# A decoder step on one core: sampled tokens' attention inside the prompt attention's loop, by pairs of heads

## The chip, the cores and the metric

The kernel runs on one core of one Trainium2 chip. TensorE (PE) multiplies and transposes, VectorE (DVE), ScalarE (ACT) and GpSimd (POOL) work elementwise, and DMAs are asked for by SyncE (SP) or, after the change, by ACT too. The time is the device time of one execution in microseconds; three executions are shown. An operand in float32 is split into a high and a low part in a rounded format (fp32r), and a product is three matmuls (high by high, low by high, high by low).

## The reference, cut to what matters

Two token sets go through the same trunk of two layers: a prompt (1024 tokens) and samples (8 sequences of 8 new tokens, each with 1024 past tokens in 8 pages of 128). Layer A is a gated short convolution. Then shared keys and values are made, and layer B attends with 16 heads of 64. For the samples, the past keys and values stand in a pool of pages that a table points into:

```python
k_past = cache_k[page_table].reshape(db, -1, N_HEADS, HEAD_DIM)     # 8 x 1024 x 16 x 64
s_past = einsum('bqhd,bkhd->bhqk', q, k_past) * scale + cn_q + rest # cn, rest: sums of log f
s_new  = einsum('bqhd,bkhd->bhqk', q, k_new) * scale + cn_q - cn    # causal, 8 x 8
p = softmax(concatenate([s_past, s_new])); o = p[..., :P] @ v_past + p[..., P:] @ v_new
```

The prompt's attention is causal over 1024 keys with a bias from the cumulated log forget values. Both results are gated by silu(z), go through w_out and a last gated feed, and a norm.

## The kernel before, in words

TT = 1088 columns are 1024 prompt tokens and 64 sampled ones, and a dense tile (one 128-wide slice of a weight matrix against all 1088 columns) is 24 pieces of three matmuls each: three column blocks (BLK) by eight slices of the inner dimension.

- **Convolution stage** (46 to about 425 us): `conv_layer` runs over j = 0 to 7 with four tiles each (t = 0 to 3). For each tile SP loads the raw weights (`load`, L312), POOL multiplies by the norm's gain (`gain`, L504), ACT rounds to w_hi (L991), DVE subtracts to w_lo (L1301). Weights have two buffers. w_hi of the next tile waits until the tile before the present one is finished. At t = 2 ACT also computes silu of the three blocks (L1052), after DVE has taken them out of PSUM. After that come w_out's eight tiles and the first feed.
- **Prompt attention** (757 to 1424.5 us): a loop over the 8 pairs of heads, each in two halves (one head each). The order of work is written out by hand in `STEPS`, which PE, ACT and DVE walk alike: ("S", qb) scores of query block qb against its keys, ("D", n) n dense pieces of the next pair's projections, ("N", i) transposes of the new keys or values, ("T", g, kb) transposes of probabilities, ("V", g, kb) product with the values. Each half has 48 dense pieces. S runs on PSUM banks 3 to 5, T and N on 5 and 6, V on 7, dense on 0 to 2. After S: DVE takes the row maximum (L1505), ACT the exponential (L1128), DVE the reciprocal (L1510), POOL multiplies (`normalise`, L536); T is followed by ACT's p_hi (L1136) and DVE's p_lo (L1516). In the last pair only 24 dense pieces are left of 96.
- **Sampled attention** (1424.5 to 1667.4 us): a loop over the 8 sequences (`sample_batch`). Pages are loaded whole from the cache (128 rows of 4 KB, L444 and L436) to `Kpages` and `Vpages`. For one sequence PE transposes 64 blocks of keys (L844), multiplies them with the queries (`s_scores`, L866; a float32 matmul stands as two instructions in the trace), adds the biases by 16 matmuls of 512 columns (`s_bias`, L855 to L858), transposes the probabilities (L895, L892) and multiplies by the values (`s_values`, L911). ACT and DVE take keys out of PSUM (L1238, L1632). There is no dense work beside this.
- **The end**: DVE's last product with the gate (L1687), the split of the result into high and low parts, w_out's eight tiles, the second feed, the norm and the stores.

SP's DMAs are asked for in program order on one queue; a wait on SP holds everything behind it.

## Time and profile before

| | us |
|---|---|
| median of 3 executions | 1923.3 (1920.92 to 1925.39) |
| profiled execution, its own time | 1923.05 |
| its span, first to last instruction | 1921.3 |
| PE busy | 1766.8 (92%) |
| PE weight loads busy | 1617.0 (84%) |
| DVE, ACT, POOL busy | 888.1 (46%), 692.3 (36%), 265.5 (14%) |
| mean granted clock of PE | 0.965 |

Times of rows are from the span's start. A timeline row is start, duration, engine, line, operation, output<-input and count; "[0.31 <-DVE ...]" is idle time before it and what ended it. SPq is SyncE's queue.

### The profile page before, as it was taken

To read this page: it belongs to the slowest core of one execution; us is meant where nothing else is said; L and a number is where in the kernel's file an instruction comes from. 1 tells how busy PE (TensorE), PEld (TensorE's weight loads), DVE (VectorE), ACT (ScalarE), POOL (GpSimd) and SP (SyncE) were. 2 spreads that over 40 slices of the span, in tenths; PEclk is the share of its full clock that TensorE was granted. 3 is DMA by queue.
4 is the path that set the end of the run, shared out by engine and by line. 5 is a ranking of instruction groups with operands and counts; after the bars stand their busy time and mean duration, and the time that the engine had idled before them with its cause. 6 is when DMAs were issued, how large, how long until landed. Compare 5 with 4: busy or idle time off the path is not lost.

```text
span 1921.3 us, 33244 instructions
## 1 busy us (share of the span) xinstructions
PE 1766.8 (92%) x11874; PEld 1617.0 (84%) x11874; DVE 888.1 (46%) x1433; ACT 692.3 (36%) x1150; POOL 265.5 (14%) x233
## 2 busy tenths in 40 slices
PE   6999999999999769999999999999779999899997
PEld 5999999999999659888888888888656666699997
DVE  4433333343253474555555555555444344423443
ACT  5111111121142234565655556555423233302332
POOL 4111111100000022222212222221100000000010
PEclk8999999999999889999999999999869999899998
DMA  4111111111211213110102111010326868721102
GB/s 140 46 46 45 45 45 45 45 33 44 75 42 30 104 13 103 35 57 23 56 23 78 46 34 56 24 56 23 134 94 268 304 258 329 279 75 49 41 27 93
DMA packets 163427, 161.61 MB, mean 84 GB/s; under 512 B 18188, under 2 KB 140172, under 8 KB 163126
## 3 DMA queue, kind: packets, MB, share of 16 engines
q1 hardware_dynamic: 163382, 161.03, 25.3%
q8 instruction: 26, 0.43, 0.1%
q14 instruction: 19, 0.16, 0.0%
HBM read 137.20 MB, written 23.80 MB: 84 GB/s over the span
## 4 chain that ended last, share of the span: by engine, by line
PE 74%; DVE 9%; ACT 5%; issue 5%; DVEq 3%; ACTq 2%; POOL 1%; DMA 0%; SPq 0%; POOLq 0%
PE PS L577 14%; PE PS L579 14%; PE PS L578 14%; PE PS L738 4%; PE PS L740 4%; PE PS L739 3%; PE PS L797 3%; PE PS L844 3%; PE PS L785 2%; DVE small L1505 2%; PE PS L911 2%; PE PS L768 2%; PE PS L866 2%; DVE pTl L1516 1%; PE PS L769 1%
## 5 line engine op out<-in xcount | busy, mean ns | idle before, releaser
L577 PE MATMUL PS<-Hhi,w_hi 128*128 128x364 f32 (+1 forms) x1536 | 511.9, 333 | 38.3 <-DVE Hlo L1351 35.1
L579 PE MATMUL PS<-Hhi,w_lo 128*128 128x364 f32 (+1 forms) x1536 | 509.7, 332 | 0.0
L578 PE MATMUL PS<-Hlo,w_hi 128*128 128x364 f32 (+1 forms) x1536 | 507.3, 330 | 0.0
L577 PEld LDWEIGHTS PS<-Hhi,w_hi 128*128 128x128 f32 x1536 | 293.9, 191 | 42.5 <-issue 29.1
L578 PEld LDWEIGHTS PS<-Hlo,w_hi 128*128 128x128 f32 x1536 | 293.1, 191 | 0.0
L579 PEld LDWEIGHTS PS<-Hhi,w_lo 128*128 128x128 f32 x1536 | 292.7, 191 | 0.0
L738 PE MATMUL PS<-Hhi,w_hi 128*128 128x364 f32 (+1 forms) x768 | 274.0, 357 | 0.1
L740 PE MATMUL PS<-Hhi,w_lo 128*128 128x364 f32 (+1 forms) x768 | 252.6, 329 | 0.0
L739 PE MATMUL PS<-Hlo,w_hi 128*128 128x364 f32 (+1 forms) x768 | 251.9, 328 | 0.0
L991 ACT ACTIVATE w_hi<-w_raw 128x1024 fp32r<-128x1024 f32 (+1 forms) x97 | 105.7, 1090 | 371.3 <-PE PS L579 368.1
L504 POOL TENSOR_TENSOR w_raw<-w_raw,GT 128x1024 f32<-128x1024 f32 x65 | 127.1, 1957 | 697.9 <-DMA w_raw<-in_w_kv 386.3
L1301 DVE TENSOR_TENSOR w_lo<-w_raw,w_hi 128x1024 fp32r<-128x1024 f32 (+1 forms) x97 | 125.2, 1290 | 79.3 <-ACT w_hi L991 76.4
L1516 DVE TENSOR_TENSOR pTl<-PS,pTh 128x512 fp32r<-128x512 f32 x192 | 103.6, 555 | 123.1 <-ACT pTh L1136 120.8
L1128 ACT ACTIVATE Pb<-PS,small 128x128 f32<-128x128 f32 (+7 forms) x128 | 94.9, 742 | 160.8 <-DVE small L1505 160.8
L536 POOL TENSOR_SCALAR Pb<-Pb,small 128x128 f32<-128x128 f32 (+7 forms) x128 | 95.6, 751 | 377.9 <-DVE small L1510 377.9
L738 PEld LDWEIGHTS PS<-Hhi,w_hi 128*128 128x128 f32 x768 | 147.0, 191 | 0.7 <-DVE w_lo L1301 0.2
L739 PEld LDWEIGHTS PS<-Hlo,w_hi 128*128 128x128 f32 x768 | 145.9, 190 | 0.0
L740 PEld LDWEIGHTS PS<-Hhi,w_lo 128*128 128x128 f32 x768 | 144.8, 189 | 0.0
L1136 ACT ACTIVATE pTh<-PS 128x512 fp32r<-128x512 f32 x192 | 89.9, 488 | 97.0 <-PE PS L785 93.7
L1505 DVE TENSOR_REDUCE small<-PS 128x1 f32<-128x128 f32 (+7 forms) x128 | 95.7, 749 | 37.2 <-PE PS L771 36.9
L797 PE MATMUL PS<-pTh,VS 128*128 128x512 f32 x192 | 73.6, 383 | 35.2 <-DVE pTl L1516 35.2
L785 PE MATMUL PS<-ident,Pb 128*128 128x128 f32 x576 | 94.7, 285 | 6.7 <-POOL Pb L536 6.7
(254 smaller groups left out, 2303.4 us busy)
## 6 DMA issues: line engine op xcount, KB each, us to landing
Kpages<-in_cache_k SPq DMA_DIRECT2D x64, 512.0 KB, 5.8
Vpages<-in_cache_v SPq DMA_DIRECT2D x64, 512.0 KB, 5.6
w_raw<-in_w_in_a SPq DMA_DIRECT2D x64, 256.0 KB, 3.0
w_raw<-in_w_ple_gate SPq DMA_DIRECT2D x16, 512.0 KB, 3.7
w_raw<-in_w_kv SPq DMA_DIRECT2D x32, 256.0 KB, 3.2
w_raw<-in_w_in_b SPq DMA_DIRECT2D x32, 256.0 KB, 3.2
parked_x<-X SPq DMA_DIRECT2D x8, 544.0 KB, 5.0
X<-parked_x SPq DMA_DIRECT2D x8, 544.0 KB, 7.8
```

What stands on the lines that cost most here:

```text
L504: g.tensor_tensor(w, w, GT[:, :, r:r + 1].to_broadcast([P, KC, P]), ALU.mult).then_inc(sems["w_gained"], 1)
L577: mm(out, wh, hi[:, k, s:e], start=(k == 0), stop=False)
L578: mm(out, wh, lo[:, k, s:e], start=False, stop=False)
L579: last = mm(out, wl, hi[:, k, s:e], start=False, stop=(k == nk - 1))
L738: mm(out, wh, Hhi[:, k, s:e], start=(k == 0), stop=False)
L739: mm(out, wh, Hlo[:, k, s:e], start=False, stop=False)
L740: last = mm(out, wl, Hhi[:, k, s:e], start=False, stop=(k == KC - 1))
L785: last = tp(PS[:, 5 + kb % 2, qi * P:(qi + 1) * P], Pb[:, off:off + P], ident[:, :])
L797: last = mm(PS[:, 7, q0 * P:512], VS[:, kb, hh, :], x[:, kb % 2, q0 * P:512], start=(kb == 0 and x is pTh), stop=(kb == nkb - 1 and x is pTl))
L1301: tt_(wlo[:, par, 0:nk, :], raw[:, par, 0:nk, :], f(whi[:, par, 0:nk, :]), ALU.subtract).then_inc(sems["w_split"], 1)
L1505: ve.reduce_max(small[:, qb:qb + 1], score_bank(qb)[:, 0:n], AXX, negate=True).then_inc(sems["rowmax"], 1)
L1516: tt_(pTl[:, kb % 2, q0 * P:512], PS[:, 5 + kb % 2, q0 * P:512], f(pTh[:, kb % 2, q0 * P:512]), ALU.subtract).then_inc(sems["p_lo"], 1)
```

## The change

1. The loop over the 8 sequences is gone. Each turn of the prompt's loop over pairs is now: half 0, a **key phase**, half 1, a **value phase**. These serve one pair of heads for all 8 sequences, so that 8 x 2 x 8 = 128 rows of scores stand in one PSUM tile of 1088 columns.
2. The 96 dense pieces of a pair are shared out anew: half 0 has 40, the key phase 12, half 1 has 38, the value phase 6.
3. The pages are first copied within DRAM, sorted by pair: keys_by_pair and values_by_pair. These 128 copies (512 KB each, in runs of 512 B) are asked for by ACT, four in each of the 32 tiles of the convolution stage, before that tile's w_hi. The loop then reads them through a ring of three buffers of 512 KB: 8 units of keys and 8 of values in a pair.
4. The biases become one matmul over 50 rows. These rows are put together by small DMAs into the tile KA for each pair.
5. The weights' buffers have another layout (parity inside), rsb and rs2 share space, the log forget values are reordered on POOL, and the end takes the prompt's result from DRAM into Hlo.

```diff
-STEPS = [("S", 0), ("D", 2), ("N", 0), ("N", 1), ("D", 1), ("S", 1), ("D", 2), ("N", 2), ("D", 1), ("S", 2), ("D", 3),
-         ("S", 3), ("D", 3), ("S", 4), ("D", 4), ("T", 0, 0), ("T", 0, 1), ("S", 5), ("D", 5), ...
+HALF0 = half_steps((2, 1, 2, 2, 3, 4, 5), (0, 1), (6, 1, 4))
+HALF1 = half_steps((2, 1, 2, 2, 3, 4, 5), (1, 2), (5, 1, 3))
+KEY_D = [1, 1, 2, 1, 2, 1, 2, 2]
+VALUE_D = [2, 4]
+RING = 3
...
+            def copy_pages(j, t):                                   # ACT
+                for pg in (2 * t, 2 * t + 1):
+                    v = act.value_load(pt[0:1, bass.ds(PAGES * j + pg, 1)], min_val=0, max_val=last_page)
+                    rows = bass.ds(v * PAGE, PAGE)
+                    by_pair = lambda x: x[rows, :].rearrange("t (j c) -> t j c", j=NPAIR)
+                    act.dma_start(dk[:, pg // 2 * P:(pg // 2 + 1) * P, bass.ds(j, 1), pg % 2, :]..., by_pair(ck)).then_inc(sems["pages_in"], 16)
+                    act.dma_start(dv[:, pg * P:(pg + 1) * P, bass.ds(j, 1), :]..., by_pair(cv)).then_inc(sems["pages_in"], 16)
             def conv_layer(j, last, first=False):
                 for t in range(4):
+                    copy_pages(j, t)
                     if last and t == 3:
...
+            def load_unit(j, u):                                    # SP
+                if u >= RING:
+                    if u - RING < PAGES:
+                        sp.wait_ge(sems["s_kturn1"], 8 * j + u - RING + 1)
+                    else:
+                        sp.wait_ge(sems["s_vused"], 8 * j + u - RING - PAGES + 1)
...
+                sp.dma_start(dst, src).then_inc(sems[f"r_in{SLOT[u]}"], 16)
+            def keys(j, more):                                      # SP, between half0 and half1
+                for u in range(RING, PAGES):
+                    load_unit(j, u)
+                if more:
                     load_b1(j, 3, 1)
...
+                for u in range(PAGES, PAGES + RING):
+                    load_unit(j, u)
+            def values(j, more):                                    # SP, after half1 and its store of yT
+                for u in range(PAGES + RING, 2 * PAGES):
+                    load_unit(j, u)
+                if more:
+                    sp.wait_ge(sems["s_vused"], 8 * j + 8)
+                    for u in range(RING):
+                        load_unit(j + 1, u)
...
+            def key_phase(j, more):                                 # PE
+                q = Q_KEYS
+                s_bias(j)                                           # 2 matmuls, 50 rows x 512 columns
+                for u in range(PAGES):
+                    s_turn(j, u)                                    # 8 transposes
+                    if u:
+                        s_scores(j, u - 1)                          # 4 matmuls of 256 columns
+                    dense(j, q, KEY_D[u], more)
+                    q += KEY_D[u]
+                s_scores(j, PAGES - 1)
+                s_new(j)                                            # 1 + 8 matmuls of 64 columns
+            def value_phase(j, more):
+                pe.wait_ge(sems["exp"], START["exp"] + 16 * j + 16)
+                pe.wait_ge(sems["s_exp"], j + 1)
...                                                                  # 8 + 1 transposes of Ps
+                dense(j, Q_VALUES, VALUE_D[0], more)
+                pe.wait_ge(sems["s_pt0"], 2 * j + 2)
+                for pg in range(PAGES):
...
+                    pe.wait_ge(sems[f"r_in{SLOT[u]}"], 16 * (USES[SLOT[u]] * j + USE[u] + 1))
+                    for g_ in range(4):
+                        last = mm(PS[32 * g_:32 * g_ + 32, 6, 0:256], PsT[:, pg, 32 * g_:32 * g_ + 32],
+                                  ring[:, SLOT[u], 256 * g_:256 * g_ + 256], start=(pg == 0), stop=False)
+                    last.then_inc(sems["s_vused"], 1)
...                                                                  # 8 matmuls with the new values
+                dense(j, Q_VALUES + VALUE_D[0], VALUE_D[1], more)
+                pe.wait_ge(sems["s_osb"], j + 1)
+                tp(PS[:, 7, 0:P], Osb, ident[:, :]).then_inc(sems["s_yturn"], 1)
...
                 if i == 0:                                          # PE, turn_part
                     pe.wait_ge(sems["staged"], 3 * j + (1, 3)[t])
+                    if t == 0 and attend:
+                        pe.wait_ge(sems["s_exp"], j)
...
+            # ACT: key_phase takes banks 3 out to KT, then Exp over 1088 columns; value_phase takes out PsT
+            # DVE: key_phase takes bank 4 out to KT, then reduce_max over 1088 columns; value_phase PsT, Osb, zsS
-            sample_batch(b, more) on PE, ACT, DVE, value_pages and Kpages loads on SP: removed
```

## Rows read from the trace of the kernel before

**Rows 1.** Busy time by stage; columns: stretch, its length, engines, clock, DMA share, GB/s.

```profile
46.00:515.00 469.00, 462.48 (x2765) 461.56 (x2765) 175.15 (x265) 64.61 (x79) 55.68 (x29) 0.99 0.16 47
757.10:1348.70 591.60, 558.14 (x3434) 505.19 (x3433) 334.16 (x601) 341.75 (x620) 134.56 (x139) 1.00 0.15 43
1348.70:1424.50 75.80, 55.18 (x246) 43.22 (x244) 34.87 (x71) 32.50 (x67) 11.97 (x16) 0.73 0.24 85
1424.50:1667.40 242.90, 220.00 (x2672) 148.05 (x2672) 102.80 (x238) 73.44 (x153) 0.00 (x0) 0.98 0.75 283
1095.10:1179.60 84.50, 79.69 (x492) 72.14 (x491) 47.80 (x87) 49.07 (x89) 19.48 (x20) 1.00 0.15 45
```

**Rows 2.** SP's timeline: stores of yT at the ends of pairs 0 and 6.

```profile
841.59 0.39 SPq L409 DMA_DIRECT2D parked_y<-yT  x1
...
1348.69 0.39 SPq L409 DMA_DIRECT2D parked_y<-yT  x1
```

**Rows 3.** PE's timeline: dense pieces, one every three matmuls.

```profile
1102.98 0.32 PE L738 MATMUL PS<-Hhi,w_hi 128*128 128x364 f32 x1
...
1103.47 0.33 PE L738 MATMUL PS<-Hhi,w_hi 128*128 128x364 f32 x1
```

**Rows 4.** PE's timeline in the sampled attention: transposes and scores of keys.

```profile
1504.38 1.07 PE L866 MATMUL PS<-KT,qc 128*32 128x256 f32 x16 [0.31 <-DVE KT L1632]
...
1526.97 1.09 PE L844 MATMUL PS<-ident,Kpages 128*128 128x128 f32 x8
1527.99 0.64 PE L866 MATMUL PS<-KT,qc 128*32 128x256 f32 x8
```

**Rows 5.** The whole timeline there: new keys, values, biases.

```profile
1506.10 0.32 PE L880 MATMUL PS<-knT,qc 128*32 128x64 f32 x8
...
1514.13 1.95 PE L911 MATMUL PS<-Vpages,PsT 128*32 128x128 f32 x64
...
1519.45 0.48 PE L855 MATMUL PS<-RT,pick 128*128 128x512 f32 x1
...
1524.73 0.44 PE L919 MATMUL PS<-ident,Osb 128*128 128x128 f32 x2
```

**Rows 6.** ACT's and DVE's timelines there: maximum, exponential.

```profile
1507.67 1.22 DVE L1658 TENSOR_REDUCE small<-PS 128x1 f32<-128x1024 f32 x1
1509.15 1.12 ACT L1252 ACTIVATE Ps<-PS,small 128x1024 f32<-128x1024 f32 x1 [0.46 <-DVE small L1660]
```

**Rows 7.** One half: exponentials on ACT, the scores on PE that wait for them.

```profile
1112.45 1.01 ACT L1128 ACTIVATE Pb<-PS,small 128x896 f32<-128x896 f32 x1 [2.41 <-DVE small L1505]
1113.61 0.50 PE L768 MATMUL PS<-KA,QA 128*128 128x512 f32 x1
```

**Rows 8.** Who waited on PE in 1095.1 to 1179.6: us, times, longest.

```profile
PE PS L797 <- DVE pTl L1516: 4.3, 5, 1.8
```

**Rows 9.** The tile Vpages: DMA (512 KB, 4 KB rows) from issue to landing.

```profile
DMA to landing us min/median/max: 3.2/5.6/7.8
```

**Rows 10.** DMA rate in 735.8 to 741, stores of KN in 512 B runs (40 slices).

```profile
GB/s 0 0 0 0 0 0 0 114 303 295 288 295 288 288 291 288 295 288 288 288 252 217 178 32 0 0 0 0 0 0 0 0 0 0 0 0 126 0 0 0
```

**Rows 11.** DMA rate in 841.5 to 847, at its end weights in 512 B runs.

```profile
GB/s 0 0 0 0 0 0 0 417 447 387 387 477 328 387 238 477 268 71 127 182 253 313 320 246 209 257 328 335 350 350 343 331 339 346 346 343 324 343 320 331
```

**Rows 12.** Line 354, eight stores of 544 KB asked for in a row: ns min/median/max.

```profile
L354 SPq DMA_DIRECT2D parked_x<-X x8: 345/1194/1237, 656.1 to 662.8; - x8
```

**Rows 13.** ACT's timeline in the convolution stage: silu and w_hi of successive tiles.

```profile
77.41 0.51 ACT L1052 ACTIVATE scrZ<-scrZ 128x360 f32<-128x360 f32 x1 [2.85 <-DVE scrZ L1379]
...
88.79 1.06 ACT L991 ACTIVATE w_hi<-w_raw 128x1024 fp32r<-128x1024 f32 x1 [9.93 <-PE PS L579]
100.75 1.06 ACT L991 ACTIVATE w_hi<-w_raw 128x1024 fp32r<-128x1024 f32 x1 [10.89 <-PE PS L579]
```

**Rows 14.** Stretches of 5 us in the last pair (columns as in rows 1).

```profile
1369.00:1374.00 5.00, 1.17 (x6) 1.03 (x7) 2.98 (x7) 3.04 (x4) 2.14 (x2) 0.68 0.95 274
...
1389.00:1394.00 5.00, 3.41 (x13) 2.51 (x13) 1.83 (x6) 1.45 (x4) 1.77 (x3) 0.50 0.00 0
```

More of the change, by code:

```diff
@@ L418, in _ @@
             load_b1(0, 3)
+            sp.wait_ge(sems["out_dma"], 32)
+            sp.wait_ge(sems["pages_in"], 16 * 2 * DB * PAGES)
+            for u in range(RING):
+                load_unit(0, u)
             store_kv(0, 0)
@@ L799, in pv_step, with dense @@
                 last.then_inc(sems["pv"], 1)
+            def dense(j, q, n, more):
+                for x in range(q, q + n):
+                    if more or x < 24:
+                        dense_piece(j, *divmod(x, PIECES))
             def half_pair(j, half, more):
-                p = 0
-                for step in STEPS:
+                q = (0, Q_HALF1)[half]
+                for step in (HALF0, HALF1)[half]:
                     if step[0] == "S":
@@ L1186, in beside @@
                 i = 2 * half + p // 24
+                if not more and half == 1 and p == 10:
+                    w_hi(N_B2 % 2, B_B2 - 3, loaded(N_B2))
                 if p % 24 == 16 and more:
@@ L1206, in beside, with dense @@
                     evacuate(j, half, *leaves[half][p], attend)
+            def dense(j, q, n, more):
+                for x in range(q, q + n):
+                    beside(j, *divmod(x, PIECES), True, more)
             def half_pair(j, half, more):
-                p = 0
-                for step in STEPS:
+                q = (0, Q_HALF1)[half]
+                for step in (HALF0, HALF1)[half]:
                     if step[0] == "S":
@@ new lines, in _ @@
+            with act.Fori(0, NPAIR - 1) as j:
+                pair(j, True)
+            pair(NPAIR - 1, False)
+            act.wait_ge(sems["o_done"], START["o_done"] + 4 * NPAIR)
+            act.wait_ge(sems["s_out"], START["s_out"] + NPAIR)
+            act.wait_ge(sems["y_back"], 16 * (KC - 1))
+            af(Hhi[:, :, SEQ:], zsS[:, :, :], ACT.Copy)
+            for k in range(KC):
+                af(Hhi[:, k, 0:SEQ], f(Hlo[:, k, 0:SEQ]) if k < KC - 1 else yT[:, 0:SEQ], ACT.Copy).then_inc(sems["h_hi"], 1)
@@ L1588, in beside, with dense @@
                     ve.tensor_copy(at_pair(zsS, j).rearrange("p a n -> p (a n)"), zf[:, SEQ:])
+            def dense(j, q, n, more):
+                for x in range(q, q + n):
+                    beside(j, *divmod(x, PIECES), True, more)
             def half_pair(j, half, more):
-                p = 0
-                for step in STEPS:
+                q = (0, Q_HALF1)[half]
+                last_sum = False
+                for step in (HALF0, HALF1)[half]:
                     if step[0] == "S":
@@ L1605, in half_pair @@
                     if step[0] == "D":
-                        for _ in range(step[1]):
-                            beside(j, half, p, True, more)
-                            if p == 29:
-                                row_sum(j, half, 7)
-                            p += 1
+                        early = 3 if last_sum else step[1]
+                        dense(j, q, early, more)
+                        if last_sum:
+                            row_sum(j, half, 7)
+                            last_sum = False
@@ new lines, in half_pair, with key_phase @@
+                        dense(j, q + early, step[1] - early, more)
+                        q += step[1]
+            def key_phase(j, more):
+                q = Q_KEYS
+                for u in range(PAGES):
+                    ve.wait_ge(sems["s_kturn1"], 8 * j + u + 1)
+                    if u >= 2:
+                        ve.wait_ge(sems["s_score"], 8 * j + u - 1)
+                    ve.tensor_copy(KT[:, u % 2, 2:4, :].rearrange("p g n -> p (g n)"), PS[:, 4, :]).then_inc(sems["s_kt1"], 1)
+                    dense(j, q, KEY_D[u], more)
+                    q += KEY_D[u]
+                ve.wait_ge(sems["s_all"], j + 1)
+                ve.reduce_max(small[:, 24:25], SS, AXX, negate=True).then_inc(sems["s_max"], 1)
```

644 lines of the change are left out of this document (296 added, 348 removed).

## The prediction

> **What bounds the kernel now.** I read the busy times by stage first, since a mean over the span says nothing of where the change acts. In the loop over pairs PE is busy for 79.7 of each turn's 84.5 us at the full clock [rows 1]; six turns lie between the stores of 841.59 and 1348.69, which makes 84.5 each [rows 2]. The other engines are at 60% or less there, so PE bounds it, with a little lost where probabilities come late: 4.3 us in five waits for DVE's pTl [rows 8]. The last pair lacks three quarters of its dense work and still takes 75.8 us, at a mean clock of 0.73: it is bound by the chain score, maximum, exponential, normalisation, transposes [rows 1]. The sampled attention takes 242.9 us, of which PE is busy 220.0, and the DMA engines work at 283 GB/s [rows 1]. So what goes away is not a gap: most of it is PE's work, which comes back inside a loop where PE has no room. The gain can come only from doing that work in fewer instructions, and from what is left of 242.9 that was no work.
>
> The sum is made against the profiled execution's own 1923.05 us (span 1921.3, 1.75 around it). The median of the three runs is 1923.3, so both stand for the same time, and the sum's result can be read against the median. A measurement of this kernel can tell about 0.2% (3.8 us) from no change.
>
> **Removed.** The whole stage from the last yT store to the last product on zsS: 242.9 us [rows 1]. The split, w_out and the rest behind it are the same work from the same starting point, so I cost the end at nothing; what would make it late is the result of the last pair, which is in the term for that pair.
>
> **PE's work added to each pair.** Eight units of eight transposes take 1.02 us each with the wait between their halves (1526.97 to 1527.99), and the eight score instructions behind them 0.5 us (16 take 1.07) [rows 4]: 8 x 1.5 = 12.0. The bias was 16 matmuls of 512 columns in 5.3 us (1519.45 to 1524.73), 0.33 each; two are left: 0.7. The new keys are one matmul and 16 instructions of 64 columns, 8 of which take 0.32: 0.6. Nine transposes of probabilities at 1.02 / 8 each: 1.1. The values were 64 instructions of 128 columns in 1.95 us; now they are 64 of 256 columns, for which the nearest row is that of the scores, 0.067 each: 4.2 us, and the new values 16 at 0.03: 0.5 [rows 4, 5]. The last transpose is 0.1. The dense pieces remain 96, at 0.49 each [rows 3], but stand in ten more groups, and the first matmul after another kind starts slower; I take 0.05 to 0.1 for each, up to 1. Together 12.0 + 0.7 + 0.6 + 1.1 + 4.2 + 0.5 + 0.1 + 0.6 = 19.8 us, against 242.9 / 8 = 30.4 that a sequence took before.
>
> **Waits added to each pair.**
> - *The ring in the value phase.* Units 8 to 10 are there. Unit 11 is asked for only when unit 8 has been used, and no dense piece stands between the units. A 512 KB load of 4 KB rows lands 3.2 us after its issue at best [rows 9], and at some 415 GB/s successive ones are 1.25 us apart. With 0.5 us of matmuls per unit and 0.35 from their end to the issue: unit 8 used at 0.5, so 11 lands at 4.05; 12 at 5.3; 13 at 6.55; 14, whose slot comes free at 4.55, at 8.15; 15 (slot free at 5.8) at 9.4. The values end at 9.9 instead of 4.0: 5.9 us of waiting. It can't be below 0. If every load takes Vpages' median of 5.6, unit 14 lands at 12.9 and unit 15 at 14.6, which makes 11 of waiting. I take 5.9, because three loads in flight are nearer to the shortest than to the queue of eight in which that median arose.
> - *The halves have 78 dense pieces instead of 96.* They covered the chain just so: the exponential of 896 columns ended at 1113.46 and the scores that wait for it began at 1113.61 [rows 7]. One piece fewer before it makes 0.4 us of wait; the same at about three places in each half makes 2.5 us. Between 0, since z's silu now comes behind the last exponential, and 9 (18 pieces of 0.49, if nothing of them was spare).
> - *Before half 1's N steps* PE waits for the sampled exponential: the maximum of 1088 columns (1.22 for 1024), the exponential (1.12) and the hand-overs [rows 6] make 3.3 us, of which S, D2, S, D1 cover 2.2. I take 1.2 (0 to 3). Behind the waiting N stand scores and dense pieces.
> - *The key phase* itself: ACT and DVE also have w_hi and w_lo there, and each key tile comes out of PSUM in 0.7 us beside 1.0 of PE's scores and dense: 0.7 (0 to 4).
> - *The clock.* In the value phase PE has work for 4.7 of 10.6 us. In 1369 to 1374 it worked 1.17 of 5 us, and the granted clock fell to 0.5 (1.2 GHz) and was still there at 1389 with 3.41 of 5 [rows 14]. I take 1.0 per pair (0 to 4).
>
> A pair then takes 84.5 + 19.8 + 5.9 + 2.5 + 1.2 + 0.7 + 1.0 = 115.6 us. Seven of them add 7 x 31.1 = 218. SP does its loads in order: the yT store and the first three units of the next pair now stand before the weights of the next dense tile, but these land some 7 us after the value phase begins to release slots and are wanted only at piece 16 of half 0, so I put nothing for them (0 to 2).
>
> **The last pair** gets no cover: a key phase of 8 x 1.6 + 1.3 = 14, a value phase of 1.2 + 1.1 + 10.4 + 2 for Osb and its transpose = 15, 3 us by which half 1's chain starts later, and 3 more at the lower clock: +35 (27 to 43).
>
> Loop and stage together: 218 + 35 - 243 = +10. The small stages (POOL's reordering, four more DMAs for the bias rows, a few DVE operations at 718) run while PE has dense tiles or the log-forget chain holds it: +1 (0 to 4).
>
> **The copies in the convolution stage.** A tile there lasts 11.96 us (w_hi at 88.79 and at 100.75 [rows 13]), and PE is busy for 462.5 of 469 us [rows 1], so this stage has no slack of its own. Each tile gets four copies of 512 KB in runs of 512 B on both sides. No row shows a DRAM to DRAM copy. From below, it is as fast as stores in such runs, 288 GB/s [rows 10]: 1.82 us. From above, reading (343 GB/s [rows 11], 1.53 us) and writing add up: 3.35 us. The weights take 0.16 of the DMA engines [rows 1], 1.9 us of a tile. So a tile's DMA time is between 9.2 and 15.3 us, and 11.96 is reached at 2.5 us a copy. The middle, 2.6, gives 12.3. ACT asks for the copies ahead of w_hi; an issue is held when the queue is full: stores of 544 KB took 0.35 us the first time and 1.19 at the median [rows 12]. In every fourth tile ACT first waits for the last silu, which ends at 77.9, 1.1 us after a tile's start (88.8 less 11.96) [rows 13]; four held issues of 2.6, w_hi 1.06 and w_lo 1.2 then end 14 us into a tile of 12. That is 2 us in each of eight turns, partly the same time as the 0.35 of each tile. I take +20 for the stage (0 to +110, which is 32 x 3.4). I choose near the middle because nothing speaks for either end.
>
> The Trainium skill's page "DMA: Bandwidth & Descriptors", section "Latency and other measured facts", gives 207 to 214 GB/s per direction for copies within HBM with 16 KB rows, with a loss at row pitches of large powers of two; by it a copy of 512 KB would take 2.45 us even with long rows, and the stage would just fit or lose a little. No run here shows such a copy. The same page ("Issuing engines are not separate DMA queues") says that asking from another engine saves only issue time; by that rule the copies on ACT's queue take their share from the weights on SP's, which is how the term above was made, and speaks against hoping for a second queue's bandwidth.
>
> **Sum:** 1923 + 10 + 1 + 20 = 1954 us.
>
> **Rivals.**
> - *A. The forecast*, 1954 (own range 1928 to 1985): chance 0.34.
> - *B. The copies bound the convolution stage.* Reads and writes add up, 3.4 us more in each of 32 tiles: 1923 + 11 + 110 = 2044. For it: the stage is full, and stores are held on issue [rows 1, 12]. Against it: 288 to 343 GB/s for each side alone [rows 10, 11]. Chance 0.22.
> - *C. Faster: the waits stay hidden.* One mechanism, in the loop: the dense pieces moved into the key and value phases stand where waits were anyway, and the value ring's loads come in time, so that only some 5 us of the 11.3 of waits are seen, the last pair adds 28 and the copies fit. A pair is 109.3: 7 x 24.8 + 28 + 1 - 243 = -40, 1883 us. It decides from a pair below 84.5 + (243 - 35 - 1) / 7 = 114.1 on, with the copies hidden; the forecast lies only 1.5 us above that. Chance 0.33.
> - *D. No change*: a pair of 114 and hidden copies, 1923. Chance 0.06.
> - *E. The clock stays low* after each value phase and the next half begins at 1.2 GHz: 4 us more a pair and 10 in the last: 1954 + 38 = 1992. Chance 0.05.
>
> **How the numbers follow.** A is likeliest: 1954. Faster is C: 0.33; same is D: 0.06; slower is A, B and E: 0.61. The range of 8 in 10 leaves out the lower third of C and the upper part of B: 1880 to 2050.
>
> **What would show it.** Right: stores of yT 115 to 116 us apart; in the value phase PE waiting for DMAs of the ring, 5 to 6 us a pair; PE's busy time in such a pair about 100 us; no row of the sampled loop after the last pair; w_hi in the convolution stage up to 1 us further apart than 11.96, with the DMA share near 0.9. Wrong: w_hi still 11.96 apart and yT below 114 (then C), or w_hi 15 us apart and ACT's issues held for 3 us (then B). The forecast fails as a whole if the value units' loads land before PE wants them, or if one copy takes more than 3 us of all engines.

## The result: 9.8% slower, and the profile after

The changed kernel takes 2110.4 us (median of 4, 2108.0 to 2113.7) against 1922.1 beside it: ratio 1.098, 95% interval 1.0955 to 1.1005. The forecast was 1954 with 1880 to 2050, so the sign was right and the size was not. The profiled execution has a span of 2112.0 us.

The stages of the changed kernel, in the columns of [rows 1]: the convolution stage, the six turns between yT's stores, the last pair up to the load of X, and one turn.

```profile
46.00:545.00 499.00, 398.50 (x2242) 390.77 (x2240) 150.74 (x229) 49.94 (x66) 59.66 (x37) 0.92 0.97 168
978.30:1726.90 748.60, 645.07 (x4370) 528.67 (x4366) 352.42 (x625) 335.58 (x606) 127.89 (x120) 0.92 0.31 100
1726.90:1855.30 128.40, 89.55 (x583) 61.04 (x575) 48.92 (x98) 41.11 (x83) 11.93 (x16) 0.78 0.40 133
1228.50:1354.10 125.60, 107.81 (x733) 88.53 (x728) 59.40 (x105) 56.08 (x102) 21.37 (x20) 0.92 0.32 99
```

The DMA engines are busy for 0.97 of the convolution stage at only 168 GB/s, where [rows 1] had 0.16 and 47; PE is busy for 80% of it, where it was 99%. In the loop PE is still the busiest, but its clock is 0.92 instead of 1.00.

Where the time went can be cut at three marks of SP's timeline: the first store of logf (709.38 before), the first and last store of yT [rows 2], and the load of X behind the last pair.

```profile
828.66 0.38 SPq L392 DMA_DIRECT2D out_logf_prompt<-lfn  x1
...
1228.53 0.39 SPq L484 DMA_DIRECT2D parked_y<-yT  x1
...
1855.29 0.80 SPq L533 DMA_DIRECT2D X<-parked_x  x2
```

| stretch | before | after | more |
|---|---|---|---|
| up to logf's store | 709.4 | 828.7 | +119.3 |
| from there to the first yT | 132.2 | 149.7 | +17.5 |
| six turns | 507.1 (84.5 each) | 748.5 (124.8 each) | +241.4 |
| last pair | 75.8 | 128.4 | +52.6 |
| sampled stage | 242.9 | 0 | -242.9 |
| the end | 253.9 | 256.7 | +2.8 |

That is +190.7 of span. The parts that change are the copies (+119 where the sum had +20) and the loop (+311 where it had +253). The cuts fall otherwise than in the kernel before: yT's store is now issued at the start of a value phase, so the stretch to the first store has no value phase, a turn has one, and the last stretch has two (those of pairs 6 and 7). The first and the last stretch can be read only together: +70.1.

ACT's timeline in the convolution stage, to set against [rows 13]:

```profile
153.89 1.98 ACTq L1112 DMA_DIRECT2D values_by_pair<-in_cache_v  x1
156.72 3.30 ACTq L1110 DMA_DIRECT2D keys_by_pair<-in_cache_k  x1
160.24 4.02 ACTq L1112 DMA_DIRECT2D values_by_pair<-in_cache_v  x1
164.44 1.06 ACT L1052 ACTIVATE w_hi<-w_raw 128x1024 fp32r<-128x1024 f32 x1 [12.83 <-issue]
...
178.62 1.06 ACT L1052 ACTIVATE w_hi<-w_raw 128x1024 fp32r<-128x1024 f32 x1 [8.29 <-issue]
```

A w_hi comes 14 us after the one before, not 12, and what ended ACT's idle time is its own issue: the asking for a copy is held for 2 to 4 us. From 151 to 296 us they are 13.3 to 16.5 us apart, 14.5 on average. This is what the prediction had given as the sign of its rival B.

The first w_hi behind the first copies is late by much more. ACT asks for eight copies ahead of it, those of two tiles, and it comes at 86.56 where the kernel before had it at 60.23; PE waits for its w_lo:

```profile
77.56 2.60 ACTq L1110 DMA_DIRECT2D keys_by_pair<-in_cache_k  x1
80.25 6.21 ACTq L1112 DMA_DIRECT2D values_by_pair<-in_cache_v  x1
86.56 1.06 ACT L1052 ACTIVATE w_hi<-w_raw 128x1024 fp32r<-128x1024 f32 x1 [27.04 <-issue]
```

```profile
88.93 0.67 PE L667 MATMUL PS<-Hhi,w_hi 128*128 128x364 f32 x1 [29.78 <-DVE w_lo L1367]
```

So 26.3 of the 119.3 us are there before the third tile begins, and the other 93 are 3.1 us in each of the 30 tiles from there on. The DMA engines have no pause in all this time (columns as in [rows 1]):

```profile
60.00:530.00 470.00, 380.90 (x2135) 373.86 (x2136) 143.97 (x218) 44.27 (x55) 58.71 (x36) 0.92 1.00 173
```

One value phase on PE's timeline, three of the eight units first and then the five that the ring still had to fetch:

```profile
1227.61 1.50 PE L983 MATMUL PS<-ring,Pb 128*32 128x256 f32 x24 [0.51 <-ACT Pb L1320]
1234.24 1.08 PE L983 MATMUL PS<-ring,Pb 128*32 128x256 f32 x8 [5.12 <-DMA ring<-values_by_pair]
1235.49 1.08 PE L983 MATMUL PS<-ring,Pb 128*32 128x256 f32 x8 [0.17 <-DMA ring<-values_by_pair]
1236.73 1.08 PE L983 MATMUL PS<-ring,Pb 128*32 128x256 f32 x8 [0.16 <-DMA ring<-values_by_pair]
1239.24 1.08 PE L983 MATMUL PS<-ring,Pb 128*32 128x256 f32 x8 [1.42 <-DMA ring<-values_by_pair]
1240.87 1.08 PE L983 MATMUL PS<-ring,Pb 128*32 128x256 f32 x8 [0.55 <-DMA ring<-values_by_pair]
```

The waits add up to 7.4 us. But a unit also lasts 1.08 us behind the gap instead of 0.5 to 0.6: the clock has fallen. The same stretch by windows of 3 us (columns as in [rows 1]; the clock is the third number from the end):

```profile
1228.00:1231.00 3.00, 1.12 (x24) 0.39 (x12) 1.32 (x4) 0.50 (x1) 0.00 (x0) 1.00 0.57 182
1231.00:1234.00 3.00, 0.00 (x0) 0.00 (x0) 0.00 (x0) 0.00 (x0) 0.00 (x0) 0.68 0.94 296
1234.00:1237.00 3.00, 2.43 (x20) 0.61 (x24) 0.00 (x0) 0.00 (x0) 0.00 (x0) 0.50 0.70 254
...
1243.00:1246.00 3.00, 3.00 (x11) 3.00 (x12) 2.19 (x5) 0.36 (x1) 0.00 (x0) 0.55 0.77 241
1246.00:1249.00 3.00, 3.00 (x24) 2.95 (x23) 1.44 (x5) 2.51 (x6) 0.00 (x0) 1.00 0.91 278
...
1255.00:1258.00 3.00, 1.57 (x6) 1.39 (x6) 0.80 (x3) 1.14 (x3) 2.47 (x5) 0.66 0.34 100
1258.00:1261.00 3.00, 3.00 (x12) 2.92 (x12) 0.82 (x1) 0.89 (x2) 1.35 (x1) 0.50 0.00 0
```

PE stood still in 1229 to 1234 and was at 1.2 GHz (0.50 in the column) until 1245.7, through dense pieces as well, then once more from 1256 to 1262.8, behind a wait of 2.7 us for an exponential.

### The profile page after: what moved, and what is told of

It reads as the page before. It is cut to its first block, busy times and chain, and to the rows that moved or that the text cites. A ratio compares the mean times of both kernels' runs of the same rounds, so it can differ in the third digit from the quotient of the medians.

```text
span 2112.0 us, 31725 instructions
## 1 busy us (share of the span) xinstructions
PE 1789.8 (85%) x11098; PEld 1610.0 (76%) x11098; DVE 878.5 (42%) x1346; ACT 674.7 (32%) x1096; POOL 287.1 (14%) x244
## 3 DMA queue, kind: packets, MB, share of 16 engines
q10 hardware_dynamic: 133120, 67.12, 19.0%
## 4 chain that ended last, share of the span: by engine, by line
PE 51%; ACTq 20%; DVE 9%; issue 7%; ACT 6%; DMA 5%; POOL 1%; DVEq 1%; SPq 1%; POOLq 0%
ACTq L1112 11%; PE PS L667 8%; PE PS L668 8%; PE PS L669 8%; ACTq L1110 6%; PE PS L828 5%; PE PS L829 4%; PE PS L830 4%; DMA ring<-values_by_pair 4%; PE PS L891 3%; PE PS L877 3%; PE PS L926 2%; DVE small L1586 2%; ACT w_hi L1052 2%; PE PS L942 2%
## 5 line engine op out<-in xcount | busy, mean ns | idle before, releaser
L667 PE MATMUL PS<-Hhi,w_hi 128*128 128x364 f32 (+1 forms) x1536 | 523.7, 341 | 130.8 <-DVE w_lo L1367 89.9
L668 PE MATMUL PS<-Hlo,w_hi 128*128 128x364 f32 (+1 forms) x1536 | 517.8, 337 | 0.0
L669 PE MATMUL PS<-Hhi,w_lo 128*128 128x364 f32 (+1 forms) x1536 | 517.2, 337 | 0.0
L667 PEld LDWEIGHTS PS<-Hhi,w_hi 128*128 128x128 f32 x1536 | 300.5, 196 | 142.5 <-issue 99.8
L668 PEld LDWEIGHTS PS<-Hlo,w_hi 128*128 128x128 f32 x1536 | 300.9, 196 | 0.0
L669 PEld LDWEIGHTS PS<-Hhi,w_lo 128*128 128x128 f32 x1536 | 299.8, 195 | 0.0
L1367 DVE TENSOR_TENSOR w_lo<-w_raw,w_hi 128x1024 fp32r<-128x1024 f32 (+1 forms) x97 | 134.2, 1383 | 382.6 <-ACT w_hi L1052 380.3
L828 PE MATMUL PS<-Hhi,w_hi 128*128 128x364 f32 (+1 forms) x768 | 289.6, 377 | 0.1
L829 PE MATMUL PS<-Hlo,w_hi 128*128 128x364 f32 (+1 forms) x768 | 260.1, 339 | 0.0
L830 PE MATMUL PS<-Hhi,w_lo 128*128 128x364 f32 (+1 forms) x768 | 259.0, 337 | 0.0
L613 POOL TENSOR_SCALAR Pb<-Pb,small 128x128 f32<-128x128 f32 (+7 forms) x128 | 106.6, 834 | 560.3 <-DVE small L1591 560.3
L828 PEld LDWEIGHTS PS<-Hhi,w_hi 128*128 128x128 f32 x768 | 152.7, 199 | 23.8 <-issue 22.9
L829 PEld LDWEIGHTS PS<-Hlo,w_hi 128*128 128x128 f32 x768 | 152.1, 198 | 0.0
L830 PEld LDWEIGHTS PS<-Hhi,w_lo 128*128 128x128 f32 x768 | 150.9, 197 | 0.0
L983 PE MATMUL PS<-ring,Pb 128*32 128x256 f32 x512 | 54.3, 531 | 64.1 <-DMA ring<-values_by_pair 59.9
```

The lines of the kernel that those rows point to most:

```text
L667: mm(out, wh, hi[:, k, s:e], start=(k == 0), stop=False)
L668: mm(out, wh, lo[:, k, s:e], start=False, stop=False)
L669: last = mm(out, wl, hi[:, k, s:e], start=False, stop=(k == nk - 1))
L828: mm(out, wh, Hhi[:, k, s:e], start=(k == 0), stop=False)
L829: mm(out, wh, Hlo[:, k, s:e], start=False, stop=False)
L830: last = mm(out, wl, Hhi[:, k, s:e], start=False, stop=(k == KC - 1))
```

## The experiments

The results first. The ratio is to the kernel before, run beside it; the last columns are the mean turn between yT's stores and logf's store in the profiled execution.

| run | us | ratio to before (95%) | turn | logf |
|---|---|---|---|---|
| changed kernel | 2110.4 | 1.098 (1.0955 to 1.1005) | 124.8 | 828.7 |
| e1 no copies | 1998.6 | 1.040 (1.038 to 1.042) | 125.8 | 711.3 |
| e2 whole pages | 2006.7 | 1.045 (1.043 to 1.048) | 124.7 | 718.8 |
| e3 before, with copies | 2041.0 | 1.062 (1.061 to 1.064) | 84.5 | 828.6 |
| e4 value units half loaded | 2006.7 | 1.048 (1.043 to 1.053) | 110.8 | |
| e5 dense in the wait | 2106.6 | 1.097 (1.095 to 1.099) | 123.4 | |
| e6 six value slots | 2063.6 | 1.073 (1.071 to 1.076) | 117.8 | |
| e7 copies spread | 2010.5 | 1.047 (1.044 to 1.050) | 124.6 | 723.6 |
| e8 e6 and e7 | 1957.6 | 1.019 (1.017 to 1.021) | 117.7 | |
| e9 e8, store behind units | 1945.4 | 1.013 (1.011 to 1.015) | 115.5 | 723.9 |
| e10 changed, store behind units | 2115.7 | 1.101 (1.100 to 1.103) | 123.7 | |
| e11 long writes | 2009.9 | 1.047 (1.045 to 1.049) | 124.8 | |
| e12 e9, copies behind w_hi | 1931.0 | 1.006 (1.005 to 1.007) | 115.4 | 711.1 |
| e13 long reads | 2103.2 | 1.094 (1.086 to 1.102) | 126.5 | 813.0 |
| e14 padded rows | 1996.2 | 1.039 (1.036 to 1.042) | 122.9 | 721.1 |
| e15 e12, padded rows | 1932.3 | 1.005 (1.003 to 1.007) | 115.7 | 710.8 |

### The copies: e1, e2, e3, e7

e1:

```diff
-                    copy_pages(j, t)
-            sp.wait_ge(sems["pages_in"], 16 * 2 * DB * PAGES)
-  src = dv[pair, (u - PAGES) * P:(u - PAGES + 1) * P, :, :]...      # keys alike
+  src = cv[bass.ds(1024 * j + (u - PAGES) * P, P), :]
```

> Leaves out: the copies of the pages by pair, and SP's wait for them; the ring is loaded in the same shapes (keys in runs of 1 KB, values in rows of 4 KB) straight from the page pool, so the numbers attended to are others. Theory R (the copies' rate bounds the convolution stage: the stage ends some 119 us later than before, logf's store at 828.7 against 709.4): 2110 - 119 = 1991 us, w_hi 12.0 us apart again. Theory L (most of the loss is in the loop and the stage of the convolution is late for another reason, such as the new layout of w_raw and w_hi by tile, or the loads): at most 20 us less, 2090. Theory G (the loop gains nothing from the missing copies): yT's stores stay 124 to 126 us apart under R and L alike.

It took 1998.6 us, 112 less, and logf's store is back at 711.31. L's 20 us is refuted: the loss in front of the loop is the copies. R's 1991 is missed by 8 us, as a turn is 1.0 us longer here (125.8), where the ring loads from other places.

e3 puts `copy_pages` as it stands into the kernel before:

```diff
             def conv_layer(j, last, first=False):
                 for t in range(4):
+                    copy_pages(j, t)
```

> The kernel before with the same copies added on ScalarE's queue in the convolution stage, their result unused; the end waits for them. The disputed cost by itself. Theory R: the stage takes 119 us more, 1922 + 119 = 2041 us. Theory of the forecast: +20, 1943. If the new layout of the weights' tiles and the sampled work's preparation share in the 119 us, it lies between, by as much as they share.

It costs 121.6 us, and logf's store comes at 828.61, within 0.05 us of the changed kernel's. So the copies alone make all of the 119.3; the weights' new layout and the sampled preparation have no share in it; without any copies (e1) they leave logf's store 1.9 us later than before.

e2:

```diff
-  act.dma_start(dv[:, pg * P:(pg + 1) * P, bass.ds(j, 1), :].rearrange("j t b c -> t j (b c)"), by_pair(cv))
+  act.dma_start(dvp[bass.ds(8 * j + pg, 1)].rearrange("a t c -> (a t) c"), cv[rows, :])      # keys alike
```

> The same number of bytes and of copies from ScalarE's queue at the same places, but each page is copied as it stands, in rows of 4 KB on both sides; the pages are not put by pair, so the numbers attended to are others. Theory D (the price is that of 133120 short packets of 512 B): the copies fit under the tiles as they would at 288 GB/s or better, 1990 to 2010 us, w_hi 12 to 12.5 us apart. Theory V (the price is that of the volume, read and written in DRAM, whatever the runs' length): 2100 to 2115, w_hi 14 to 15 us apart.

2006.7 us: it is not the volume. From here I took it to be the packets of 512 B, which e11 and e14 below correct.

e7 (the helper `copies` asks for numbers x of a sequence's sixteen):

```diff
-                    copy_pages(j, t)
+                    copies(j, (0, 2, 5, 7)[t], (2, 5, 7, 10)[t])
     # in each of w_out's and the first feed's tiles:
+                    copies(i, 10 + 3 * u, 13 + 3 * u)
```

> The changed kernel with the same 128 copies of 512 B runs, asked for two or three in each tile of the convolution stage (ten of each sequence's sixteen) and three in each of the 16 tiles of w_out and the feed behind it; nothing is left out. Theory R (a copy of such runs costs 3.07 us of all 16 DMA engines: 83.2% of 473 us by 128; three and the weights are 9.2 + 2.5 = 11.7 us, just under a tile of 11.96): the 112 to 122 us go, 1995 to 2010 us. Theory H (it is the hold of ScalarE's issues, which comes back wherever copies stand): 2040 to 2100, with w_hi later than 12 us in the tiles with three.

2010.5 us, 100 less, within R's 1995 to 2010 but for 0.5. Logf's store is still 12.3 us later than in e1, and there is one long wait in front of it: PE stands 16.4 us for w_lo until 75.8 us, right behind the first copies, where it stood 29.8 in the changed kernel. e12 takes this up.

### What makes a copy dear: e11, e13, e14

e11 writes a page's eight column blocks one behind the other; e13 reads them so and writes in the places of the changed kernel; e14 is the complete changed kernel with an unused ninth sequence in each row:

```diff
-  dk = nc.dram_tensor("keys_by_pair", (NPAIR, 4 * P + 1, DB, 2, P), ...)
-  dv = nc.dram_tensor("values_by_pair", (NPAIR, 8 * P + 1, DB, P), ...)
+  dk = nc.dram_tensor("keys_by_pair", (NPAIR, 4 * P + 1, DB + 1, 2, P), ...)
+  dv = nc.dram_tensor("values_by_pair", (NPAIR, 8 * P + 1, DB + 1, P), ...)
```

> The changed kernel with the same 128 copies, which read runs of 512 B as before, but write each page's eight columns one behind the other (64 KB without a gap for each pair), so that only the side that is read has gaps; the ring reads the tensors in the same shapes, so the numbers attended to are others. Theory D (the price is per packet of 512 B, whichever side makes it): 2100 to 2115 us, w_hi 14 to 15 us apart. Theory E (the scattered writes are the dear part): under 2050, w_hi nearer to 12.

> The changed kernel with the 128 copies turned round: they read each page in eight pieces of 64 KB without a gap and write them in the places of the changed kernel (runs of 512 B, a row of 4 KB or 8 KB from one to the next), so the numbers attended to are others. The run with the long side on the writes took 2009.9 us, 1.8 us of all DMA engines a copy; the changed kernel with short runs on both sides 3.1. Theory WR (scattered writes are the dear part): still 3 us a copy, 2095 to 2115 us, w_hi 14 to 15 us apart. Theory BO (it needs gaps on both sides to be slow): under 2030 us.

> The changed kernel, complete, with one more unused sequence in each row of keys_by_pair and values_by_pair: the copies write runs of 512 B at a pitch of 4.5 KB and 9 KB from one token to the next, where it was 4 KB and 8 KB; the pieces read are the same. Theory PI (the writes are slow because their pitch is a power of two, so that they meet in the same places of the memory): 2 us a copy, under 2040 us. Theory SH (it is the shortness of the runs that are written, whatever their pitch): 2100 to 2120 us.

The DMA queue of the copies (q10) in 60 to 430 us, in the changed kernel, e11, e13 and e14; columns: packets, MB, share of 16 engines.

```profile
q10 hardware_dynamic: 103696, 52.29, 83.6%
```

```profile
q10 hardware_dynamic: 130548, 65.82, 61.6%
```

```profile
q10 hardware_dynamic: 107067, 53.98, 87.6%
```

```profile
q10 hardware_dynamic: 130860, 65.98, 60.7%
```

A copy has 1040 packets (133120 by 128), so one costs 0.836 x 370 / 99.7 = 3.10 us of all engines in the changed kernel, 1.82 in e11, 3.15 in e13 and 1.79 in e14; whole pages (e2) 1.44. D is refuted by e11: the packets are as many and as short, and the time is 100 us less. (In e13 logf's store still comes 15.7 us earlier than in the changed kernel, 813.0 against 828.7; that was not followed.) E, WR and then PI's time hold: what is dear is the writing of 512 B runs in the places of the changed kernel, at a pitch of exactly 4 KB (values) or 8 KB (keys) from token to token. With 4.5 and 9 KB the same 512 B runs, in as many packets and in a complete kernel, cost 42% less and the stage nearly hides them: 1996.2 us. The unused sequence also moves the eight pairs of a page further apart: from 4 MiB and 4 KB (values: 1025 tokens of 4 KB) or 4 MiB and 8 KB (keys: 513 of 8 KB) to about 4.5 MiB. No run changes one of the two distances alone. Shown is that the distances between the written runs decide; which of the two does, and that the writes meet in the same places of the memory, as PI has it, was not seen.

The Trainium skill's page "DMA: Bandwidth & Descriptors", section "Latency and other measured facts", has such a rule: a pitch that is a large power of two slows copies within HBM, and padding the rows restores them. e14 agrees that padding helps (1.79 us a copy instead of 3.10). If the pitch from token to token is what counts, it does so at a far smaller pitch than the page's 512 KiB and more, and with a smaller pad (512 B and 1 KB). The page's 207 to 214 GB/s, from which 2.45 us a copy is an estimate, is below what e2 shows (1.44 us of the engines' time, 364 GB/s each way).

### The value phase: e4, e5, e6, e10

e4:

```diff
-                for u in range(PAGES + RING, 2 * PAGES):
-                    load_unit(j, u)
+                    if pg < RING:      # PE waits for units 8 to 10 only
                         pe.wait_ge(sems[f"r_in{SLOT[u]}"], ...)
```

> Leaves out the loads of value units 11 to 15 (their products use what the ring's slots hold). It takes away the ring's waits in the value phase and nothing else. The profile of the changed kernel shows 59.9 us of waits there. Theory W (only the waits): 7.5 us a pair, 2110 - 60 = 2050 us. Theory K (the wait also costs the clock: PE at 1.2 GHz for 1234 to 1245 and again for 1256 to 1262.5): 10 to 12 us a pair, 2110 - 90 = 2020. Theory F (other waits take its place, as the exponential for half 0's scores): 3 to 5 us a pair, 2080.

2006.7 us, 13.9 a turn less, more than K's upper end. Its six turns, and one of them:

```profile
975.74:1640.77 665.03, 608.84 (x4369) 512.99 (x4362) 346.66 (x625) 335.11 (x606) 124.10 (x120) 0.99 0.28 88
1309.60:1419.70 110.10, 100.52 (x731) 84.77 (x727) 57.75 (x105) 55.82 (x101) 20.88 (x20) 1.00 0.29 89
```

In this turn PE is busy for 100.5 us at the full clock, where the turn shown of the changed kernel needs 107.8 for the same instructions. Over six turns the busy time is 608.8 instead of 645.1: 6.0 us a turn are clock. The other 7.9 are waits. (The run also loads 2.6 MB less in a turn, which was not separated.)

e5 and e10 are one move each: the four dense pieces up behind the third unit; the yT store behind the loads of units 11 to 15.

```diff
+                    if pg == RING - 1:
+                        dense(j, Q_VALUES + VALUE_D[0], VALUE_D[1], more)
-                dense(j, Q_VALUES + VALUE_D[0], VALUE_D[1], more)      # behind the last value
```

> The changed kernel with one move on TensorE: the four dense pieces behind the value units (before Osb's transpose) stand behind the third value unit, where PE waits for the ring; nothing is left out. Theory W (only the wait counts): the 2.1 us of pieces go under the wait of 5.1 us, but Osb's two steps on DVE (some 1.5 us) and its transpose lose their cover, so 0.6 us a pair or nothing, 2105 to 2110 us. Theory K (the wait also drops PE's granted clock to 1.2 GHz): PE's gap is 3 us instead of 5.1; if that keeps the clock at full, some 4 to 6 us a pair more come back, 2065 to 2080. If the clock falls in the shorter gap too, K gives the same as W.

2106.6 us: W, or K with a clock that falls in the shorter gap too. The longest wait fell from 5.9 to 3.6 us and the waits for values from 59.9 to 47.7, yet the clock fell as before, and Osb's transpose now waits 1.0 us a pair. The time can't be told from no change.

> The changed kernel with the store of yT asked for behind the value units 11 to 15 instead of ahead of them (three slots as in the changed kernel); nothing else. In the changed kernel the store is issued at 1228.53 and the first unit at 1229.17, with the slot free at 1228.1, and the 512 KB of the store go through the same DMA engines (1.4 to 1.8 us at 296 to 377 GB/s). Theory Q (part of the ring's wait is the store ahead of it): 2 us of waits a pair and perhaps 1 of low clock, 2110 - 20 = 2090 us. Theory N (latency of each load bounds the ring, the store does not count): 2105 to 2112.

2115.7 us, a little above N's 2112 and not clear of the changed kernel's 2110.4; waits of 59.7 us as before: N. The longest wait got shorter (3.3) while the sum stayed. With three slots, the time from a load's issue to its landing (4.5 us in the median) is what is left to explain it; that was not changed by itself.

e6:

```diff
+SLOTS = RING + 3
+BETWEEN = {4: 1, 5: 1}      # a dense piece behind units 12 and 13
+SLOT = [u % RING for u in range(PAGES)] + [2, 0, 1, 3, 4, 5, 2, 0]
+slots = [ring[:, r, :] for r in range(RING)] + [Pb[:, c:c + D] for c in (0, D, 2 * D + 9 * P)]
+                    elif u < PAGES + SLOTS:
+                        sp.wait_ge(sems["turned"], START["turned"] + 24 * j + (21, 21, 23)[u - PAGES - RING])
```

> The changed kernel with three more slots for value units, in parts of the probabilities' tile that half 1 has done with (loaded from its fifth and seventh turn on), and one dense piece behind each of the value units 12 and 13; nothing is left out, the copies stay. Theory K, after the run without the loads of units 11 to 15 (2006.7 us, 13.9 us a pair less): the waits and the low clock both go, 2006 to 2015 us, yT's stores 110 to 112 us apart. Theory F (the loads now collide with what SP does at the end of half 1, or the yT store and its users come later): 2030 to 2070. PE's work is the same in both.

2063.6 us: 47 us, a little under half of what e4 gave. F: units 14 and 15 are asked for behind the store of yT, and in the last pair behind seven loads of Hlo, where PE waits 9.2 us. The clock still fell, though later.

### Together: e8, e9, e12, e15

> Both: the copies spread and six slots for the value units; nothing is left out. If the two losses are separate, 2110 - 112 - 103 = 1895 us, which would be faster than the kernel before (1919 to 1923) by 1.3%. Theory S (the losses share something, so that the second comes back in part): 1915 to 1940.

1957.6 us, outside both theories. The two gains add up (100 + 47 = 147 of 153); the 1895 was wrong because e6 gave 47, not 103, and S's sharing is not seen.

e9 (in the loop, and the last pair's order):

```diff
-  half1:  ... sp.dma_start(d["y"]..., yT[:, 0:SEQ])
+  values: load_unit(14), load_unit(15), sp.dma_start(d["y"]..., yT[:, 0:SEQ])
+  last pair: the loads of Hlo ahead of load_unit(11 to 13)
```

> The version with spread copies and six value slots (1957.6 us), with two changes of order on SP's queue: the store of yT (512 KB) is asked for behind the value units 14 and 15 instead of ahead of them, and in the last pair the seven loads of Hlo (3.6 MB) ahead of the units 11 to 13 instead of between these and 14. Nothing is left out. In that version PE still waits 2.2 us a pair and 10 in the last for the last two units, and the granted clock falls to 0.5 for some 7 us behind. Theory K (what is missing against the run without loads, 111 a pair, is this wait and this clock): 1957 - 7 x 6 - 9 = 1906 us, faster than before. Theory P (PE's thin work in this stretch, 24 products and transposes with gaps for ScalarE's copies, drops the clock in any case): 1935 to 1945.

1945.4 us: P's time (1935 to 1945), far from K's 1906. With six slots the same move that was worth nothing in e10 gives 2.2 us a turn; the other move, that of Hlo's loads, goes with 12 in the last stretch. P's "in any case" does not hold: in two of six turns the clock stays at 1.00 (113.3 us), in the others it still falls and they take 115 to 119. One turn of each kind, and the longest gaps of PE at its start:

```profile
1108.40:1221.70 113.30, 101.77 (x735) 84.31 (x727) 57.63 (x104) 55.75 (x101) 21.22 (x20) 1.00 0.34 109
1221.70:1340.60 118.90, 105.95 (x735) 88.63 (x727) 59.19 (x104) 56.09 (x101) 21.38 (x20) 0.96 0.33 104
```

```profile
1112.75 0.64 PE L993 MATMUL PS<-ring,Pb 128*32 128x256 f32 x8 [1.27 <-DMA ring<-values_by_pair]
...
1224.64 0.64 PE L993 MATMUL PS<-ring,Pb 128*32 128x256 f32 x8 [0.72 <-DMA ring<-values_by_pair]
1226.00 0.64 PE L993 MATMUL PS<-ring,Pb 128*32 128x256 f32 x8 [0.72 <-DMA ring<-values_by_pair]
```

The clock stayed at 1.00 behind the longer gap and fell at 1231.6 behind the two shorter ones. The later gaps are alike (0.43 and 0.95 us in the one turn, 0.41 and 0.97 in the other), so the longest gap alone does not tell which turn is slow.

e12:

```diff
                         w_hi((t + 1) % 2, 12 * j + 3 * t, gained=4 * j + t + 2)
+                    if not (first and t == 0):
+                        copies(j, 0 if first and t == 1 else (0, 2, 5, 7)[t], (2, 5, 7, 10)[t])
-HALF0 = half_steps((2, 1, 2, 2, 3, 4, 5), (0, 1), (6, 1, 4))
+HALF0 = half_steps((2, 2, 3, 2, 4, 4, 5), (0, 1), (5, 1, 4))
-KEY_D = [1, 1, 2, 1, 2, 1, 2, 2]
+KEY_D = [1, 1, 1, 1, 1, 1, 2, 2]
```

> The version of 1945.4 us with two more changes of place; nothing is left out. (1) ScalarE asks for the two or three copies of a tile behind the tile's w_hi instead of ahead of it. In that version the third to fifth copy are held on issue for 3.9, 4.1 and 4.6 us ahead of the first w_hi (73.84 us), PE waits 16.2 us for w_lo there, and logf's store stands at 723.93 us against 711.31 without copies. Theory H (that is the hold of the issue, and what is behind it waits): logf's store at 711 to 715, 9 to 13 us less. Theory M (it is the DMA engines' load on the weights, which stays): under 4 us less. (2) Two dense pieces move from the key phase to half 0's turns 1 and 2, and one from the last turn to turn 4, where PE waits 2.4 us for an exponential and 1.9 us for POOL. Theory T: 2 us a pair (yT's stores 113 to 114 apart), 14 to 16 us in all; its rival: the waits only move to the key phase, 0. With H and T 1918 us, equal to the kernel before; with M and no T 1943.

1931.0 us. The start of its convolution stage on ACT:

```profile
59.20 1.06 ACT L1064 ACTIVATE w_hi<-w_raw 128x1024 fp32r<-128x1024 f32 x1
60.02 0.74 ACTq L1124 DMA_DIRECT2D keys_by_pair<-in_cache_k  x1
...
64.05 2.99 ACTq L1127 DMA_DIRECT2D values_by_pair<-in_cache_v  x1
67.74 5.62 ACTq L1124 DMA_DIRECT2D keys_by_pair<-in_cache_k  x1
73.46 1.06 ACT L1064 ACTIVATE w_hi<-w_raw 128x1024 fp32r<-128x1024 f32 x1 [13.20 <-PE PS L678]
```

Issues are held as long as before, but the second w_hi now waits for PE and not for them, and logf's store is at 711.13: H, 12.8 us. T is refuted: a turn is 115.4 instead of 115.5; the three pieces saved nothing.

> The version of 1931.0 us (copies spread and behind w_hi, six value slots, the store of yT behind the value units, three dense pieces moved) with the pitch of 4.5 KB and 9 KB in the two tensors; complete. In the version of 1931.0 the stages up to logf's store are already within 2 us of the kernel before (711.13 against 709.38), so a faster copy has nothing more to hide there: theory A2 (the copies were all that the pitch cost) 1928 to 1932 us. Theory B2 (the ring's loads, which read at the same pitch, come sooner or more evenly too: a pair took 122.9 us with the pitch alone, 124.8 without): 1.5 us a pair less, 1915 to 1920, even with the kernel before or just faster.

1932.3 us, the same as e12: A2. The pitch costs nothing that can be seen where the ring reads, and the turn of 122.9 us in e14 (124.8 in the changed kernel; 0.5 of it in PE's busy time, 1.4 in its waits) stays unexplained. So the two best of these versions, e12 and e15, are still slower than the kernel before, by 0.5 to 0.6% (intervals 0.3 to 0.7).

## Why the prediction was wrong, by its steps

- **The copies** are the step that failed most: "I take +20 for the stage", seen +119. The form of the sum was right: one resource, 4 copies and the weights against 11.96 us, break-even at 2.5 us a copy. The size was not: 3.1 us instead of 2.6, inside the bounds of 1.82 to 3.35, and the weights' queue takes 16.4% of the engines in 60 to 430 us, 2.4 us a tile instead of 1.9. By these a tile is 4 x 3.1 + 2.4 = 14.8 us, 2.8 more than 11.96 where the sum had 0.35; seen are 3.1 in each of 30 tiles, 93 us. The other 26 stood in no term: the eight copies that ACT asks for ahead of the first w_hi. So the middle of the bounds was no estimate at all. The Trainium skill's page that the prediction cites names row pitches of large powers of two, and I weighed only its rate for long rows, not what the pitch would do to these writes; e14 shows that the price turns on where the runs are written. Rival B's place and size (+110, seen +119) were right; its mechanism, that reads and writes add up, was not: e14's copies read and write as much for 1.8 us, which is the lower bound that the stores of [rows 10] gave. That 3.1 lies near B's 3.35 is luck.
- **Issues held on ACT**: expected at 2.6 us each, seen at a median of 2.1 and 4.0 us (keys and values). In the 30 tiles, where the DMA engines are busy all the time, the sum of copies and weights already gives 2.8 of the 3.1 us, so little is left for the holding itself; with all four copies in a tile no other order was tried. Where the engines aren't the bound, the order alone costs 12.8 us (e12 against e9, at the start).
- **PE's work**, 19.8 us a pair: right. 79.7 + 19.8 = 99.5 against 100.5 in e4's turn at the full clock.
- **Waits outside the value phase** (2.5 + 1.2 + 0.7 on top of 4.8): right in sum; the single ones were not compared. In e4's turn PE is idle for 9.6 us; 9.2 were expected.
- **The ring in the value phase**, 5.9: seen 7.5 a pair (59.9 in all), within the bounds (the upper one is 10.7 by its own terms, since unit 15 lands at 14.15 there and not at 14.6). Unit 11 was used 6.6 us after the phase began (1234.24 against 1227.61), not at 4.05, since a load takes 4.5 us in the median instead of the 3.2 I chose. The yT store goes ahead of it too, but moving it (e10) left the waits as they were.
- **The clock**, 1.0 a pair: the second term that failed, outside its 0 to 4. The same instructions need 107.5 us a turn, 6.0 more than in e4 and 7.0 more than in its turn at the full clock. [Rows 14] had shown 1.2 GHz still there 15 us after a thin stretch; I priced the phase alone and not the dense work and scores behind it.
- **A turn**: 115.6 forecast, 124.8 seen. Without the ring's waits and most of the low clock (e4) it is 110.8, against 108.7 for the sum without its two terms. **The first and the last stretch** together: 31.1 + 35 = 66.1 forecast, 70.1 seen. So +35 for the last pair was nearly right: the +52.6 of its stretch holds pair 6's value phase too, which the first stretch lacks.
- **The end and the small stages** (0 and +1): the end is 2.8 later, and logf's store without copies, at 711.3, 1.9 later; 4.7 together.

In e12, with hidden copies and short ring waits, a turn is 115.4 us: about what the forecast said for the loop. The change then still loses. The loop takes 20.9 us more up to the first store, 185.6 in the six turns and 38.4 in the last stretch, together 244.9, where the sampled stage took 242.9; the front adds 1.8 and the end 2.7. PE's 19.8 us a pair, with the added idle time and what is left of the ring and the clock, is as much as the 30.4 that a sequence took before.

## What to carry to other kernels

When a resource stands at its break-even, do not choose the middle between two bounds: what decides may be the one property of the transfer that no row has, here the distances between the runs that are written; padding the rows by 512 B and 1 KB was worth 114 of 188 us. Look also at what stands ahead of the first piece of work: the first w_hi stood behind eight requests and came 26 us late. Price a wait on PE with the clock behind it, over all work that runs until it is back: here 6 us of clock on 8 of waits. PE bounded the loop and the stage that moved into it, so only fewer or shorter instructions could gain: PE's work fell from 27.5 us a sequence (220.0 / 8) to 19.8 a pair, and waits and the clock took that back. More slots for prefetch gave 47 us, and 12 more once the stores and loads ahead of theirs had been moved.

## What the runs showed of the hardware

- DRAM to DRAM, 512 KB, of all 16 DMA engines: 1.44 us for whole pages (e2), 1.8 for 512 B runs with contiguous writes (e11) or at 4.5 and 9 KB from token to token (e14), 3.1 for the same runs written at 4 and 8 KB (changed kernel, e13); gaps in the reads at a 4 KB pitch are in the 1.8 already.
- With the first copies in flight, ACT's fourth request in a row and those right behind it are held for 2.6 to 6.2 us in the changed kernel, with everything behind them on ACT; the first three take 0.6 to 0.7.
- PE's clock fell to 1.2 GHz behind thin stretches: in the changed kernel behind a gap of 5 us, in e9 behind gaps of 0.7 to 2.0 us. In the turns shown it stayed there through 3 to 6 us of full work. In e9 it fell in four of six turns with the same instructions and not in two, and these turns differ by up to 5 us.
